# A third weight chunk loaded out of turn, behind packed work buffers, in an encoder block with 32 experts

## The chip, the cores and the metric

The kernel runs on one core of one Trainium2 chip, in one launch. The metric is its time on the device in microseconds, the median of several runs. Beside it stands the hardware profile of one execution, from which all rows below are taken.

## The reference

The reference is one layer of a bidirectional encoder for 256 tokens of width 1024, in float32, cut here to what matters:

```python
h = rms_norm(x, attn_norm_g)                 # attention front
proj = h @ w_in                              # q, k, v of 8 + 12 heads, q of 4 memory heads, 3 gates
merged = gate_a*(A @ w_a) + gate_b*(B @ w_b) + gate_c*(C @ w_c)
x = x + merged @ w_out
h = rms_norm(x, ffn_norm_g)                  # expert part
top_val, top_idx = top_k(h @ router_w + router_b, 4)   # 4 of 32 experts per token
# for each expert, on the tokens that chose it:
gu = xb @ w_gu[e] + b_gu[e]                  # (1024, 2048)
g, u = minimum(gu[:, :1024], 7), clip(gu[:, 1024:], -7, 7)
y = ((u + 1) * g * sigmoid(1.702 * g)) @ w_dn[e] + b_dn[e]   # (1024, 1024)
x = rms_norm(x + sum over the chosen experts of weight * y, final_norm_g)
```

The weights of one expert are 12 MiB, those of all 32 are 384 MiB. All of them are read, whatever the tokens choose.

## The kernel before

**Front.** The weights of the attention part come in 42 chunks of 1 MiB (`NF`) through the first 6 slots of a ring of chunks. Each chunk is split into a high and a low part (ScalarE and GpSimd, `w_parts`), and TensorE (PE) multiplies three pairs of parts. After chunk 41 x is complete; the router's logits, the top 4, the ranks in each expert and the matrices that gather an expert's tokens follow.

**Experts.** One expert is 12 chunks of 1 MiB: 8 of gate and up (k = 0 to 7), 4 of down. Each expert has 64 token slots. PE does, for expert n: the bias rows; the chunks k = 0 to 3; the scatter of expert n-2's result into the four banks that hold x; the turning of the weights; k = 4, 5; a gather of later tokens; k = 6, 7; the four down chunks of expert n-1; the turning of expert n's activation. So the chunks are used in the order gate and up of n, then down of n-1 (`gate_up_chunk`, `down_chunk`, L148 to L155). `chunk_used` counts them. VectorE limits gate and up into `gate_c` and `up_c` (L1492, L1493), multiplies them (L1496, `prod_ready`), multiplies by the sigmoid (L1499), and copies the turned activation (L1501). ScalarE takes the sigmoid of `gate_c` (L1213), and copies the down sums of expert n-1 out of bank 3 into `y_sb` (`move_down`, L1215), which the scatter reads; for the last expert VectorE does this copy (L1513).

**Loads.** All weight loads are issued by SP, in one order. The ring has 20 slots of 8 KB per partition (`RING`, `CHUNK`); chunk c lies in slot (c + 8) mod 20. `TRANSFERS` (L158) groups the chunks: transfers of 2 chunks for the first experts and the last, of 4 for the gate and up chunks of experts 4 to 30, of 2 for the down chunks. A transfer of m chunks from c on is issued when PE has used chunk c - 20 + m - 1 (L534). The first 20 chunks go in before: five transfers during the front (`EARLY_AFTER`), five when the front's last chunks are used (`FIRST_LAP`); the last of these, chunk 16 (down weights of expert 0), waits for all 42 chunks of the front and stands behind four small loads of the expert biases.

**Lent places.** Two chunks of expert 5 (`LENT_TO`), its k = 6 and 7, numbers 62 and 63 (`LENT`), do not go through the ring. They are loaded in pieces of 256 KB into buffers that have become free: x (all of k = 7, since x is by then in the banks), the router's constants, the raw biases, and the routing's scratch (`lent_pieces`, L383). SP issues them between the first lap and the first load of the ring's second lap (L524 to L530, the last piece at L538). They have semaphores of their own (`lent_in`). Their ring slots stay unused in that lap, and the loads after them still wait by their own number. The down bias and the final gain go into x's place when that chunk has been used (L539 to L542), and PE adds the down bias in four matmuls during the experts 9 to 12 (`DOWN_BIAS_AT`).

**Memory.** The front's work buffers and the experts' share one arena behind the ring's first 12 slots, `FRONT_WORK` = 22784 words per partition. The front's parts of the merged tokens (`mergedHL`) lie at its end. The row maxima and the sums of the attention are tensors of their own in front of the arena (L217 to L220).

Of the kernel before, what the change touches and what calls it, by code (L numbers as in the profile page):

```python
# [25 lines left out]
P = 128  # L26
# [13 lines left out]
EXPERTS, TOP_K = 32, 4  # L40
# [7 lines left out]
CHUNK = 2048  # L48
# [3 lines left out]
SCORE_SLOT = 8  # L52
SECOND_SPLIT_SLOT = 10
FRONT_SLOT = 12
FRONT_WORK = 22784
LATE_PARTS = (39, 41)
IMAGES = 3
EXPERT_CHUNKS = 12
# [25 lines left out]
NU = len(UNITS)  # L84
# [8 lines left out]
T5_STORE_AFTER = 11  # L93
STEP_SLOT = {s: i for i, s in STEP_AFTER.items()}

DOWN_BIAS_AT = {9: (0, 0), 10: (0, 1), 11: (1, 0), 12: (1, 1)}
IMAGE_AFTER = {u: 9 if u < 2 + IMAGES else STEP_SLOT[u - IMAGES] + FRONT_RING for u in range(2, NU)}

EARLY_AFTER = {36: 0, 38: 4, 39: 6, 40: 8, 41: 10}
FIRST_LAP = {2: 38, 12: 38, 14: 40, 18: 41, 16: NF}  # L100
FIRST_LONG = 4

LENT_TO = 5
LENT = (EXPERT_CHUNKS * LENT_TO + 2, EXPERT_CHUNKS * LENT_TO + 3)

QK_DONE, QKV_DONE = {"C": 6, "A": 10, "B": 18}, {"C": 6, "A": 12, "B": 21}

# [45 lines left out]
def down_chunk(n):  # L153

    return gate_up_chunk(n + 1) + KC if n + 1 < EXPERTS else EXPERT_CHUNKS * EXPERTS - 4  # L155


def transfers():  # L158

    short, long, down = [(j, 2) for j in range(0, KC, 2)], [(0, 4), (4, 4)], [(KC, 2), (KC + 2, 2)]  # L160
    end_down = [(KC, 2), (KC + 2, 1), (KC + 3, 1)]
    order = [(0, *t) for t in short]
    for n in range(1, EXPERTS):
        lent = [(0, 4), (4, 2), (6, 1), (7, 1)]
        order += [(n, *t) for t in (lent if n == LENT_TO else long if FIRST_LONG <= n < EXPERTS - 1 else short)]
        order += [(n - 1, *t) for t in (down if n < EXPERTS - 1 else end_down)]
    order += [(EXPERTS - 1, *t) for t in end_down]
    c, out = 0, {}
    for e, j, m in order:
        out[c] = (e, j, m)  # L170
        c += m
    return out


TRANSFERS = transfers()


# [4 lines left out]
def build(nc, t):  # L182
# [4 lines left out]
    w_gu = t["expert_w_gate_up"].rearrange("l e (p a) c -> (l e) p (a c)", p=P)  # L187
# [5 lines left out]
    with ExitStack() as ctx:  # L193
        def sb(name, shape, dt=F32):
            return ctx.enter_context(nc.sbuf_tensor(name, shape, dt))
# [13 lines left out]
        until_ranked = sb("until_ranked", [P, 512])  # L209
# [4 lines left out]
        pick_raw = sb("pick_raw", [P, 2, EXPERTS + 1])  # L214
        sumsq = sb("sumsq", [P, 4, T])
        rstd = sb("rstd", [P, 4, T])
        row_max = sb("row_max", [P, NU, 4])  # L217
        neg_max = sb("neg_max", [P, 8, 4])
        exp_sum = sb("exp_sum", [P, NU, 4])
        inv_sum = sb("inv_sum", [P, 8, 4])  # L220
        ovf = sb("ovf", [P, MAX_OVERFLOW + 1], I32)
        b_tmp = sb("b_tmp", [P, 2, 4])

# [2 lines left out]
        FRONT0, MOE0 = FRONT_SLOT * CHUNK, RING * CHUNK  # L226
# [7 lines left out]
        def area(off, *dims):  # L234
            n = int(np.prod(dims))
            assert off + n <= FRONT0 + FRONT_WORK
            flat = arena[:, off:off + n]
            if len(dims) == 2:
                return flat.rearrange("p (a b) -> p a b", a=dims[0])
            if len(dims) == 3:  # L240
                return flat.rearrange("p (a b c) -> p a b c", a=dims[0], b=dims[1])
            if len(dims) == 4:
                return flat.rearrange("p (a b c d) -> p a b c d", a=dims[0], b=dims[1], c=dims[2])
            return flat
# [2 lines left out]
        pT = area(FRONT0, 2, 2, 2, S)  # L247
        image = area(FRONT0 + 2048, IMAGES, 2, IMG)
        na_mask = area(FRONT0 + 2048 + IMAGES * 2 * IMG, 4, GRID_W // 2)
        v = area(FRONT0 + 4352, T, 1280)  # L250
        mv = area(FRONT0 + 6912, T, MEM_HEADS * MEM_HD)
        qkT = area(FRONT0 + 8192, 24, S)
# [32 lines left out]
        place = [MOE0]  # L285

        def moe(*dims):
            at = place[0]
            place[0] += int(np.prod(dims))
            return area(at, *dims)  # L290
# [6 lines left out]
        gate_c, up_c = moe(512), moe(512)  # L297
# [1 line left out]
        assert place[0] <= FRONT0 + 18688  # L299
        router_parts = area(place[0], S)  # L300
        sig = moe(512)
        y_sb, aT = moe(512), moe(4, P)
        wT_sel = moe(S)[0:EXPERTS, :]
        pick = split_at("pick", place[0], 2, 2 * BLK)
        moe(2 * 2 * BLK)
        until_routed = area(place[0], 512)
# [5 lines left out]
        okeys = moe(T, EXPERTS)  # L312
        extra, ends = moe(EXPERTS), moe(EXPERTS)
        ovf_f = moe(MAX_OVERFLOW)
        final_g, far_iota, b_dn = x[:, 0, :], x[:, 1, :], x[0:EXPERTS, 1, :]
        final = xn[:]

# [4 lines left out]
        lent_in = {c: sem(f"lent_in{c}") for c in LENT}  # L322
# [36 lines left out]
        gate_ready, gu_drained, sig_ready = sem("gate_ready"), sem("gu_drained"), sem("sig_ready")  # L359
        prod_ready, act_ready = sem("prod_ready"), sem("act_ready")  # L360
# [16 lines left out]
        def front_fills(r):  # L377
# [2 lines left out]

        x_flat = x[:].rearrange("p t c -> p (t c)")
        bias_flat = bias_raw[:].rearrange("p b c -> p (b c)")
        lent_pieces = {LENT[0]: [bias_flat[:, 0:512], bias_flat[:, 512:1024], until_ranked[:], until_routed],  # L383
                       LENT[1]: [x_flat[:, 512 * i:512 * (i + 1)] for i in range(4)]}

        def piece(c, i):
# [7 lines left out]
        ALL_CHUNKS = EXPERTS * EXPERT_CHUNKS  # L394
# [37 lines left out]
        def _(sp):  # L432
# [13 lines left out]
            for i in range(NF):  # L446
# [7 lines left out]
                kind, n = FRONT[i]  # L454
                dst = ring[:, i % FRONT_RING, :]
                if i in WIDE_FIRST or i in WIDE_LAST:
                    late = int(i in WIDE_LAST)
                    first = (n - late) * SLOTS_W
                    src = {"mem": w_mem, "in": w_in}[kind][:, 4 * late:4 * late + 4, first:first + 2 * SLOTS_W]
                    dst = dst.rearrange("p (k c) -> p k c", k=4)  # L460
                elif kind in ("mem", "in", "out"):
                    src = {"mem": w_mem, "in": w_in, "out": w_out}[kind][:, :, n * SLOTS_W:(n + 1) * SLOTS_W]
                    dst = dst.rearrange("p (k c) -> p k c", k=KC)
                elif kind == "branch_b":
                    src, dst = w_br[kind], dst.rearrange("p (k c) -> p k c", k=2)
                else:
                    src, dst = w_br[kind][:, :, n * 512:(n + 1) * 512], dst.rearrange("p (k c) -> p k c", k=4)
                if i == 0:
                    sp.dma_start(dst[:, 0:KC // 2], src[:, 0:KC // 2]).then_inc(first_half_in, 16)
                    dst, src = dst[:, KC // 2:], src[:, KC // 2:]  # L470
                sp.dma_start(dst, src).then_inc(landed[i % FRONT_RING], 16)
                if i in EARLY_AFTER:
# [6 lines left out]
                    c = EARLY_AFTER[i]  # L479
# [30 lines left out]

            sp.wait_ge(merged_ready, 4)
            sp.dma_start(iota, bass.AP(t["iota"].tensor, 0, [[0, P], [1, BLK]])).then_inc(iota_in, 16)
            for c, used in FIRST_LAP.items():
                sp.wait_ge(chunk_used, used)
                if used == NF:
                    load_bias()
                load_weights(*TRANSFERS[c], ring_slot(c))
            def lend(c, first, n, place):

                e, j, _ = TRANSFERS[c]  # L520
                src = w_gu[bass.ds(e, 1), :, j * CHUNK + 512 * first:j * CHUNK + 512 * (first + n)].rearrange("o p c -> (o p) c")
                sp.dma_start(place, src).then_inc(lent_in[c], 16)

            sp.wait_ge(normed, 3)  # L524
            sp.wait_ge(tile_normed, 1)
# [51 lines left out]
        def _(pe):  # L577
# [345 lines left out]
            def weights_landed(c):  # L923

                if c in LENT:
                    pe.wait_ge(lent_in[c], {LENT[0]: 48, LENT[1]: 16}[c])
                else:
                    pe.wait_ge(landed[ring_slot(c)], 16 * fills_through(c))

# [9 lines left out]
            for n in range(EXPERTS):  # L939
# [10 lines left out]
                for k in range(KC):  # L950
                    c = gate_up_chunk(n) + k
# [47 lines left out]
            with pe.If(0 < n_over):  # L999
                with pe.Fori(0, MAX_OVERFLOW) as b:  # L1000
                    with pe.If(b < n_over):
                        n = b + EXPERTS
# [33 lines left out]
        def _(act):  # L1036
# [68 lines left out]
            for i, (kind, n) in enumerate(FRONT):  # L1105
# [13 lines left out]
                elif kind in ("mem", "in") and i not in WIDE_FIRST:  # L1119
# [5 lines left out]
                    src = ps[:, PLAIN[i] % 2, :].rearrange("p (t c) -> p t c", t=2)  # L1125
                    if kind == "mem":
                        if n < 2:
                            e = nc.scalar.copy(mkT[:, 2 * n:2 * n + 2, :], src)
                        else:
                            e = nc.scalar.copy(mv[:, :, (n - 2) * 256:(n - 1) * 256], src)  # L1130
                    elif n in Q_SCALE and n < 15:

                        e = nc.scalar.mul(qkT[:, QKT[n]:QKT[n] + 2, :].rearrange("p b (t q) -> p b t q", t=T),
                                          reversed_tiles(src), Q_SCALE[n])
                    elif n in QKT:
                        e = nc.scalar.mul(qkT[:, QKT[n]:QKT[n] + 2, :], src, Q_SCALE.get(n, 1.0))
                    elif n in V_COL:
                        e = nc.scalar.copy(v[:, :, V_COL[n]:V_COL[n] + 256], src)
                    else:
                        buf, c = GATE_BRANCH[n]  # L1140
                        e = nc.scalar.activation(gate_cols(buf, c * 256, 256), src, ACT.Sigmoid)
# [9 lines left out]
                if i in STEP_AFTER:  # L1151
# [13 lines left out]
                    if 0 <= u < NU and u == last_unit_of(OUTPUT_OF[u]):  # L1165
                        o = OUTPUT_OF[u]
                        act.wait_ge(pv_done, u + 1)
                        high, _, src = output_parts(o)
# [43 lines left out]
                act.wait_ge(gate_ready, n + 1)  # L1212
                nc.scalar.activation(sig, gate_c, ACT.Sigmoid, scale=ALPHA).then_inc(sig_ready, 1)  # L1213

            def move_down(chunks, bank):  # L1215
                act.wait_ge(chunk_used, chunks + NF)
                nc.scalar.copy(y_sb, ps[:, bank, :]).then_inc(y_ready, 1)  # L1217

            for n in range(EXPERTS):
                if n:  # L1220
                    move_weights(n - 1, (n - 1) % 2)
                if n + 2 < EXPERTS:
                    move_gathered(n % 2, XT[:, (n // 2 + 1) % 2], 2 * BLK, n + 2)
                sigmoid(n)
                if n:
                    move_down(down_chunk(n - 1) + 4, 3)
            move_weights(EXPERTS - 1, (EXPERTS - 1) % 2)
            n_over = act.value_load(ovf[0:1, MAX_OVERFLOW:MAX_OVERFLOW + 1], min_val=0, max_val=MAX_OVERFLOW)
            with act.If(0 < n_over):
                with act.Fori(0, MAX_OVERFLOW) as b:  # L1230
                    with act.If(b < n_over):
                        for half in range(2):
                            move_gathered(half, XT[:, 0], BLK, b * 2 + (EXPERTS + half))
                        move_weights(b + EXPERTS, 1)
                        sigmoid(b + EXPERTS)
                        move_down(b * EXPERT_CHUNKS + (ALL_CHUNKS + EXPERT_CHUNKS), 3)

            nc.scalar.activation(b_tmp[:, 0, 0:1], eps[:], ACT.Sqrt)
            for tt in range(T):
# [367 lines left out]
```

## Time and profile before

| | us |
|---|---|
| median of 3 runs | 1232.18 (1231.66 to 1232.54) |
| profiled execution: its own time | 1229.89 |
| profiled execution: span | 1228.1 |
| PE busy | 1174.6 (96%) |
| VectorE busy | 267.5 (22%) |
| ScalarE busy | 253.0 (21%) |
| GpSimd busy | 207.2 (17%) |
| bytes moved by DMA | 455.14 MB, mean 371 GB/s |

The span is the time from the first to the last instruction of the profiled execution. The share of busy time is a mean over the whole span, which has a front of some 305 us and an expert part of some 920 us with different limits, so it has to be read in stretches. Matmuls are pipelined and their ends are modelled: a busy PE may still wait a little inside.

### The profile page before, as it was taken

What the parts mean: (1) busy time and instruction counts of PE and PEld (TensorE: products, weight loads), DVE (VectorE), ACT (ScalarE), POOL (GpSimd) and SP (SyncE); (2) the same over time, 40 slices, a digit from 0 to 9 for tenths busy, and PEclk for the clock granted to TensorE, in tenths of its full rate; (3) what the DMA queues carried; (4) which work ended last, traced back from release to release, by engine and by line L of the source; (5) the groups of instructions that cost most, each with busy time, mean ns of one, the idle gap of its engine ahead of it and who ended that gap; (6) DMA issues with size and microseconds to landing.
All of it is one profiled execution on the core that took longest, in us unless ns stands there. A gap on an engine that the chain in (4) does not pass through costs nothing.

```text
span 1228.1 us, 14301 instructions
## 1 busy us (share of the span) xinstructions
PE 1174.6 (96%) x6225; PEld 605.9 (49%) x6225; DVE 267.5 (22%) x543; ACT 253.0 (21%) x531; POOL 207.2 (17%) x89
## 2 busy tenths in 40 slices
PE   8999999999999999999999999999998998999996
PEld 8989887899433433333333333333333333333332
DVE  3148252232411112111111121111111111111112
ACT  6446455344301011100101010000100000000101
POOL 5865766686100000000000000000000000000000
PEclk9999999999999999999999999999999999999999
DMA  9753544599999999999999999999999999999995
GB/s 316 241 168 122 167 155 137 185 357 389 347 428 430 425 430 415 430 430 429 432 432 431 428 430 431 430 429 430 433 429 431 427 432 428 430 429 427 430 427 231
DMA packets 61703, 455.14 MB, mean 371 GB/s; under 512 B 5081, under 2 KB 33657, under 8 KB 43464
## 3 DMA queue, kind: packets, MB, share of 16 engines
q1 hardware_dynamic: 61640, 454.22, 90.0%
q8 instruction: 50, 0.82, 0.3%
q14 instruction: 13, 0.11, 0.0%
HBM read 453.13 MB, written 1.07 MB: 370 GB/s over the span
## 4 chain that ended last, share of the span: by engine, by line
PE 63%; DMA 33%; DVE 1%; POOL 1%; ACT 1%; issue 0%; DVEq 0%; SPq 0%; ACTq 0%; POOLq 0%
PE ps L579 62%; DMA arena<-in_expert_w_gate_up 29%; DMA arena<-in_expert_w_down 3%; POOL w_parts L568 1%; PE ps L895 1%; PE ps L889 0%; DVE arena L1371 0%; DMA arena<-in_mem 0%; DVE x_normed L1542 0%; PE ps L702 0%; PE ps L586 0%; ACT arena L1087 0%; PE ps L679 0%; DVE arena L1401 0%; DVE arena L1267 0%
## 5 line engine op out<-in xcount | busy, mean ns | idle before, releaser
L579 PE MATMUL ps<-arena,gathered_T 128*64 128x512 f32 x2034 | 471.2, 611 | 36.3 <-DMA arena<-in_expert_w_gate_up 36.3
L579 PE MATMUL ps<-arena 128*64 128x512 f32 (+8 forms) x1650 | 335.7, 534 | 4.1 <-DVE arena L1401 1.6
L579 PEld LDWEIGHTS ps<-arena,gathered_T 128*64 128x64 f32 x2034 | 144.9, 140 | 302.0 <-issue 273.3
L579 PEld LDWEIGHTS ps<-arena 128*64 128x64 f32 (+3 forms) x1650 | 132.2, 153 | 198.9 <-issue 191.6
L568 POOL TENSOR_TENSOR w_parts<-arena,w_parts 128x1024 fp32r<-128x1024 f32 x42 | 102.9, 2474 | 46.8 <-ACT w_parts L1067 37.7
L568 POOL TENSOR_TENSOR w_parts_odd<-arena,w_parts_odd 128x1024 fp32r<-128x1024 f32 x38 | 90.8, 2409 | 45.7 <-ACT w_parts_odd L1067 45.7
L1486 DVE TENSOR_SCALAR arena<-arena 128x128 f32<-128x128 f32 x64 | 19.3, 344 | 315.3 <-PE ps L889 315.3
L1209 ACT COPY arena<-ps 128x256 f32<-128x256 f32 x32 | 11.9, 372 | 358.8 <-PE ps L889 358.8
L1492 DVE TENSOR_SCALAR arena<-ps 128x512 f32<-128x512 f32 x32 | 22.1, 692 | 273.1 <-PE ps L579 273.1
L579 PEld LDWEIGHTS ps<-arena,x_normed 128*128 128x128 f32 x512 | 59.5, 192 | 24.8 <-issue 24.3
L1200 ACT ACTIVATE gathered_T<-ps,g_cols 128x128 f32<-128x128 f32 x128 | 36.5, 368 | 170.1 <-PE ps L579 170.1
L579 PE MATMUL ps<-arena,x_normed 128*128 128x128 f32 x512 | 65.4, 281 | 0.2 <-DVE arena L1443 0.2
L579 PE MATMUL ps<-w_parts_odd,h_T_parts 128*128 128x256 f32 (+1 forms) x360 | 59.1, 322 | 0.0
L1501 DVE COPY arena<-ps 128x512 f32<-128x512 f32 x32 | 22.1, 691 | 155.1 <-PE ps L895 155.1
L579 PEld LDWEIGHTS ps<-w_parts_odd,h_T_parts 128*128 128x128 f32 x360 | 51.5, 188 | 7.1 <-issue 1.8
L1217 ACT COPY arena<-ps 128x512 f32<-128x512 f32 x31 | 18.2, 586 | 172.3 <-PE ps L579 172.3
L1067 ACT CAST w_parts<-arena 128x1024 fp32r<-128x1024 f32 x40 | 39.9, 1047 | 49.2 <-PE ps L579 49.0
L1067 ACT CAST w_parts_odd<-arena 128x1024 fp32r<-128x1024 f32 x38 | 37.9, 1047 | 40.8 <-PE ps L579 40.3
L1213 ACT ACTIVATE arena<-arena 128x512 f32<-128x512 f32 x32 | 20.3, 633 | 109.6 <-DVE arena L1492 109.6
L579 PE MATMUL ps<-w_parts,h_T_parts 128*128 128x512 f32 (+1 forms) x216 | 41.1, 347 | 0.0
L579 PEld LDWEIGHTS ps<-w_parts,h_T_parts 128*128 128x128 f32 x216 | 33.7, 188 | 6.2 <-issue 0.6
L579 PE MATMUL ps<-h_T_parts,w_parts 128*128 128x256 f32 x288 | 35.5, 282 | 0.0
(181 smaller groups left out, 727.1 us busy)
## 6 DMA issues: line engine op xcount, KB each, us to landing
arena<-in_expert_w_gate_up SPq DMA_DIRECT2D x53, 4096.0 KB, 39.4
arena<-in_expert_w_down SPq DMA_DIRECT2D x62, 2048.0 KB, 38.8
arena<-in_expert_w_gate_up SPq DMA_DIRECT2D x21, 2048.0 KB, 12.4
arena<-in_w_in SPq DMA_DIRECT2D x29, 1024.0 KB, 5.4
arena<-in_w_out SPq DMA_DIRECT2D x4, 1024.0 KB, 11.3
arena<-in_expert_w_down SPq DMA_DIRECT2D x4, 1024.0 KB, 41.0
arena<-in_w_mem_kv SPq DMA_DIRECT2D x3, 1024.0 KB, 12.3
arena<-in_w_branch_a SPq DMA_DIRECT2D x2, 1024.0 KB, 5.1
```

Source lines behind the costliest of these rows:

```text
L568: last = nc.gpsimd.tensor_tensor(parts_at(i)[:, 1, half], ring[:, i % FRONT_RING, half], parts_at(i)[:, 0, half].bitcast(F32), ALU.subtract)
L579: return nc.tensor.matmul(out, lhsT, rhs, start=start, stop=stop, **kw)
L895: last = nc.tensor.transpose(ps[:, 2, f * P:(f + 1) * P], sig.rearrange("p (q f) -> p f q", f=4)[:, f, :], ident[:])
L1067: nc.scalar.copy(parts_at(i)[:, 0, half], ring[:, i % FRONT_RING, half]).then_inc(high_ready, 1)
L1200: last = nc.scalar.mul(xt[:, c, 0:width], ps[:, bank, k * P:k * P + width], g_cols[:, 3 * KC + c:3 * KC + c + 1])
L1209: nc.scalar.copy(WT[:, wt_slot, :], ps[:, 3, 0:S]).then_inc(WT_ready, 1)
L1213: nc.scalar.activation(sig, gate_c, ACT.Sigmoid, scale=ALPHA).then_inc(sig_ready, 1)
L1217: nc.scalar.copy(y_sb, ps[:, bank, :]).then_inc(y_ready, 1)
L1486: last = vec.tensor_scalar(PW[:, tt, :].rearrange("p (a s) -> p a s", a=2), bcast(slots, 1, 2), key_tile[:, tt, e], w_sel[:, tt, e], ALU.i ...
L1492: vec.tensor_scalar(gate_c, ps[:, 0, :], LIMIT, None, ALU.min).then_inc(gate_ready, 1)
L1501: vec.tensor_copy(aT, ps[:, 2, :].rearrange("p (f s) -> p f s", f=4)).then_inc(aT_ready, 1)
```

## The change

A third chunk is lent. All three belong to expert 6, the seventh (k = 5, 6 and 7, numbers 73 to 75), and expert 5 gets all its chunks through the ring. The new one, `LENT[2]` (k = 7), is one transfer of 1 MiB into a place of its own, the last 2048 words of the arena (`behind_work`), and is issued right behind chunk 16, before SP's waits for the normed tokens. Chunk k = 4 of expert 6 is then a ring transfer of one chunk.

To make room, the arena grows by 240 words, the four tiles of row maxima and sums move into a gap of it (between the mask and the values), and the down sums `y_sb` take the buffer of `gate_c`. ScalarE's copy of the down sums waits in addition for `prod_ready` and `sig_ready`. The load of the down bias and the final gain, and its additions, move one expert later.

```diff
-FRONT_WORK = 22784
+FRONT_WORK = 23024
...
-DOWN_BIAS_AT = {9: (0, 0), 10: (0, 1), 11: (1, 0), 12: (1, 1)}
+DOWN_BIAS_AT = {10: (0, 0), 11: (0, 1), 12: (1, 0), 13: (1, 1)}
...
-LENT_TO = 5
-LENT = (EXPERT_CHUNKS * LENT_TO + 2, EXPERT_CHUNKS * LENT_TO + 3)
+LENT_TO = 6
+LENT = tuple(EXPERT_CHUNKS * LENT_TO + j for j in (1, 2, 3))
...
-        lent = [(0, 4), (4, 2), (6, 1), (7, 1)]
+        lent = [(0, 4), (4, 1), (5, 1), (6, 1), (7, 1)]
...
-        row_max = sb("row_max", [P, NU, 4])
-        neg_max = sb("neg_max", [P, 8, 4])
-        exp_sum = sb("exp_sum", [P, NU, 4])
-        inv_sum = sb("inv_sum", [P, 8, 4])
...
+        stats_at = FRONT0 + 4096
+        row_max, exp_sum = area(stats_at, NU, 4), area(stats_at + 64, NU, 4)
+        neg_max, inv_sum = area(stats_at + 128, 8, 4), area(stats_at + 192, 8, 4)
...
-        y_sb, aT = moe(512), moe(4, P)
+        y_sb, aT = gate_c, moe(4, P)
...
+        behind_work = area(FRONT0 + FRONT_WORK - CHUNK, CHUNK)
+        assert place[0] <= FRONT0 + FRONT_WORK - CHUNK
...
-        lent_pieces = {LENT[0]: [bias_flat[:, 0:512], bias_flat[:, 512:1024], until_ranked[:], until_routed],
+        lent_pieces = {LENT[2]: [behind_work[:, 512 * i:512 * (i + 1)] for i in range(4)],
+                       LENT[0]: [bias_flat[:, 0:512], bias_flat[:, 512:1024], until_ranked[:], until_routed],
...
             for c, used in FIRST_LAP.items():
                 sp.wait_ge(chunk_used, used)
                 if used == NF:
                     load_bias()
                 load_weights(*TRANSFERS[c], ring_slot(c))
+            lend(LENT[2], 0, 4, behind_work)
 
             sp.wait_ge(normed, 3)
...
-                    pe.wait_ge(lent_in[c], {LENT[0]: 48, LENT[1]: 16}[c])
+                    pe.wait_ge(lent_in[c], {LENT[0]: 48, LENT[1]: 16, LENT[2]: 16}[c])
...
-            def move_down(chunks, bank):
+            def move_down(chunks, bank, n):
                 act.wait_ge(chunk_used, chunks + NF)
+                act.wait_ge(prod_ready, n + 1)
+                act.wait_ge(sig_ready, n + 1)
                 nc.scalar.copy(y_sb, ps[:, bank, :]).then_inc(y_ready, 1)
```

## Rows read from the trace of the kernel before

**Rows 1.** The page, rate of all DMA engines in 40 slices of 30.7 us:

```profile
GB/s 316 241 168 122 167 155 137 185 357 389 347 428 430 425 430 415 430 430 429 432 432 431 428 430 431 430 429 430 433 429 431 427 432 428 430 429 427 430 427 231
```

**Rows 2.** Busy by windows: length, PE, PEld, DVE, ACT, POOL, PEclk, DMA share, GB/s.

```profile
324.00:650.00 326.00, 324.61 (x1566) 125.09 (x1564) 53.72 (x122) 34.62 (x88) 0.00 (x0) 1.00 1.01 428
650.00:1200.00 550.00, 513.30 (x2398) 196.04 (x2394) 82.70 (x183) 49.65 (x125) 0.00 (x0) 0.98 1.00 429
...
1200.00:1221.00 21.00, 19.06 (x86) 6.96 (x86) 3.65 (x6) 3.83 (x8) 0.00 (x0) 1.00 0.57 237
```

**Rows 3.** Waits of PE, in total: us, times, longest.

```profile
PE ps L579 <- DMA arena<-in_expert_w_gate_up: 36.3, 27, 2.8
...
PE ps L579 <- DMA arena<-in_expert_w_down: 1.3, 1, 1.3
```

**Rows 4.** The chain of waits that ended last: start, length, what.

```profile
440.19 0.68 PE ps L895 x4
...
466.66 0.68 PE ps L895 x4
...
649.30 37.10 DMA arena<-in_expert_w_gate_up
...
1160.60 40.15 DMA arena<-in_expert_w_down
...
1211.01 7.04 PE ps L579 x32
```

**Rows 5.** Timeline of SP, 285 to 350 us: start, length, DMA issued.

```profile
307.27 0.58 SPq L440 DMA_DIRECT2D arena<-in_expert_w_down  x1
313.76 0.33 SPq L522 DMA_DIRECT2D x_tokens<-in_expert_w_gate_up  x1
...
315.95 0.33 SPq L522 DMA_DIRECT2D bias_raw<-in_expert_w_gate_up  x1
321.51 0.33 SPq L440 DMA_DIRECT2D arena<-in_expert_w_gate_up  x1
```

**Rows 6.** Busy time by windows, around the added transfer.

```profile
307.00:314.00 7.00, 6.86 (x31) 3.74 (x30) 4.56 (x27) 5.21 (x6) 3.85 (x1) 1.00 1.00 341
...
314.00:322.20 8.20, 8.15 (x54) 5.18 (x56) 7.41 (x28) 2.28 (x8) 0.00 (x0) 1.00 0.64 240
```

**Rows 7.** Time to landing of the loads issued at 313.8, 315.9, 321.5, 380.4, 459.8.

```profile
DMA to landing us min/median/max: 4.8/4.8/4.8
...
DMA to landing us min/median/max: 4.9/4.9/4.9
...
DMA to landing us min/median/max: 7.1/7.1/7.1
...
L440 SPq DMA_DIRECT2D arena<-in_expert_w_gate_up x1: 328/328/328, 380.4 to 380.4; - x1
...
DMA to landing us min/median/max: 13.8/13.8/13.8
...
L440 SPq DMA_DIRECT2D arena<-in_expert_w_gate_up x1: 328/328/328, 459.8 to 459.8; - x1
...
DMA to landing us min/median/max: 18.6/18.6/18.6
```

**Rows 8.** Timeline near the end, ScalarE's copy and who waits.

```profile
1201.72 0.69 DVE L1499 TENSOR_TENSOR arena<-arena 128x512 f32<-128x512 f32 x1
...
1208.01 0.59 ACT L1217 COPY arena<-ps 128x512 f32<-128x512 f32 x1 [7.06 <-PE ps L579]
1208.65 0.30 PEld L579 LDWEIGHTS ps<-arena 64*128 64x128 f32 x4 [0.18 <-ACT arena L1217]
```

**Rows 9.** Timeline of PE: products behind a wait.

```profile
1098.03 7.09 PE L579 MATMUL ps<-arena,gathered_T 128*64 128x512 f32 x32 [2.35 <-DMA arena<-in_expert_w_gate_up]
...
1127.30 8.78 PE L579 MATMUL ps<-arena,gathered_T 128*64 128x512 f32 x32 [2.38 <-DMA arena<-in_expert_w_gate_up]
...
1200.89 7.09 PE L579 MATMUL ps<-arena 128*64 128x512 f32 x32 [1.33 <-DMA arena<-in_expert_w_down]
```

More of the change, by code:

```diff
@@ L512, in _, with lend @@
             sp.dma_start(iota, bass.AP(t["iota"].tensor, 0, [[0, P], [1, BLK]])).then_inc(iota_in, 16)
+            def lend(c, first, n, place):
+                e, j, _ = TRANSFERS[c]
+                src = w_gu[bass.ds(e, 1), :, j * CHUNK + 512 * first:j * CHUNK + 512 * (first + n)].rearrange("o p c -> (o p) c")
+                sp.dma_start(place, src).then_inc(lent_in[c], 16)
             for c, used in FIRST_LAP.items():
@@ L517, in _ @@
                 load_weights(*TRANSFERS[c], ring_slot(c))
[L518 to L522, printed above, removed]
+            lend(LENT[2], 0, 4, behind_work)
             sp.wait_ge(normed, 3)
@@ L1225, in _ @@
                 if n:
-                    move_down(down_chunk(n - 1) + 4, 3)
+                    move_down(down_chunk(n - 1) + 4, 3, n)
             move_weights(EXPERTS - 1, (EXPERTS - 1) % 2)
@@ L1235, in _ @@
                         sigmoid(b + EXPERTS)
-                        move_down(b * EXPERT_CHUNKS + (ALL_CHUNKS + EXPERT_CHUNKS), 3)
+                        move_down(b * EXPERT_CHUNKS + (ALL_CHUNKS + EXPERT_CHUNKS), 3, b + EXPERTS)
             nc.scalar.activation(b_tmp[:, 0, 0:1], eps[:], ACT.Sqrt)
```

## The prediction

> **What bounds the kernel now.** I read the page first. In its line of GB/s the rate is 122 to 389 in the first eleven slices (each is 30.7 us), the attention front and the routing; from the twelfth on it stays between 415 and 433, up to the last slice [rows 1]. The table by windows makes that exact: 428 GB/s at a DMA share of 1.01 from 324 to 650 us, 429 GB/s at 1.00 from 650 to 1200 us [rows 2]. So the weights of 32 experts come in one unbroken stream that begins at about 322 us. Whether this stream also sets the time is told by PE's waits: on weights of gate and up it waited 36.3 us, on weights of down 1.3 us [rows 3], and the chain of waits shows from when. Up to 649.30 us it is all PE: two successive turns of an activation stand at 440.19 and 466.66 us, so PE has a period of 26.47 us per expert, in which it frees 12 chunks. One expert of 12 MiB takes the stream 12 x 1.0486 MB / 429 GB/s = 29.3 us. PE is the quicker by 2.9 us per expert, uses up what had been loaded ahead, and from 649.30 us on the long pieces of the chain are DMA, the last of them from 1160.60 to 1200.75 us [rows 4]. What is left is PE work of fixed length: the last down products but one at 1200.89 us [rows 9], the last at 1211.01 to 1218.05 us. The end is thus the landing of expert 30's first down chunks plus some 27 us, and that landing is set by how many bytes the stream has to bring before it, since it never pauses.
>
> Two consequences. PE work before 1200 us costs nothing up to the 37.6 us that it waits. And a byte is worth its time only if it leaves the stream: it has to be moved to a time at which the queues stand empty.
>
> **The added transfer.** A third chunk of 1 MiB is taken out of the stream (72 to 75 of expert 6: one in the ring, three lent; before, two of expert 5) and is loaded by SP right behind the last load of the first lap, before SP's wait for the normed tokens. At 429 GB/s it is worth 1,048,576 / 429,000 = 2.44 us.
>
> Is there an empty place for it? The last load of the first lap (2 MiB of down weights) is issued at 307.27 us; then SP sleeps until 313.76 us, issues the lent pieces until 316.3 us, sleeps again until routing is done enough and issues the first ring load behind the lap at 321.51 us [rows 5]. The 16 DMA engines are full from 307 to 314 us (share 1.00), but from 314 to 322.2 us their share is 0.64 at 240 GB/s [rows 6]: 8.2 x 0.36 = 2.95 us of all engines stand idle, or, by bytes, (429 - 240) x 8.2 = 1.55 MB against the 1.05 MB to be put there. The new transfer would be issued at about 307.9 us and lie ready behind the 2 MiB; the pieces issued at 313.76 us and later follow it. All is done about half a microsecond before 322.2 us, when the data of the 321.51 load start. That load is released by PE (chunks 0 and 1 of expert 0 used), so it neither comes earlier nor later. I take the whole 2.44 us as hidden. The bounds: nothing hidden (the gain is 0), all hidden (2.44 us).
>
> Here the Trainium skill speaks against the change: "DMA: Bandwidth & Descriptors", section "Bandwidth", gives a transfer of 1 MB 6.15 us and 341 GB/s, and its "Anatomy of one DMA" a fixed part of about 2 us for each. By that an estimate of the new transfer is 4.4 to 6.2 us, which is 1.5 to 3.2 us more than the idle 2.95, and the sum would be between a gain of 0.9 us and a loss of 0.8 us. The trace disagrees for transfers that stand behind each other: 1 MiB issued at 313.76 us landed after 4.8 us and the 0.5 MiB issued at 315.95 us landed by 320.9 us [rows 5, 7], so three transfers with 1.75 MiB took 7.1 us in all, where three fixed parts of 2 us and the bytes would be 10.3.
>
> **The later skip.** A lent chunk leaves a hole in the ring's order: the next load still waits until PE has used the chunk 20 before it. In the hole nothing is issued, and the queue is eaten by so much. If it runs dry, the gain is lost there. The depth ahead of a transfer follows from its time to landing. On an empty queue 2 MiB took 7.1 us, of which 4.9 are bytes, so 2.2 are start and receipt. The 4 MiB issued at 380.42 us took 13.8: less 9.8 for its bytes and 2.2, 1.8 us of work stood ahead of it, and the stream did not pause. The 4 MiB issued at 459.83 us took 18.6: 6.6 us stood ahead [rows 7]. In the new kernel expert 5 brings all of its 8 gate and up chunks through the ring (2 MiB more than before, issued by 414 us), expert 6 brings 5 (3 MiB less, by 435 us). So up to the hole the queue is deeper than before, and at 459.83 us, its least, shallower by 1 MiB: 6.6 - 2.44 = 4.2 us, more than twice what sufficed at 380 us. From there PE frees chunks 2.9 us per expert faster than they arrive, and the depth grows. Cost of the skip: 0, with bounds 0 and the 6.6 us in which PE frees three chunks (3/12 of 26.47).
>
> The loads of the down bias and the final gain move one expert later with the x buffer, and so do the four additions of the bias (experts 10 to 13). These 0.6 MiB are in the full stream either way: 0. PE's additions fall before 649 us or into its slack: 0. The number of ring transfers is the same for the experts 5 and 6 together (four). SP issues one DMA more, 0.33 us in a sleep of 5.9 us [rows 5]: 0.
>
> **The moved buffers.** The four tiles of row maxima and sums go behind the work buffers of the front into a gap between the mask and the values; no wait is added, and the transfers that overwrite this place already wait for the attention's end: 0.
>
> The down sums take the buffer of the gate. ScalarE's copy then waits for two more semaphores: the product that reads the gate (VectorE) and the sigmoid. Queued behind the copy on ScalarE are the next weights' copy and gather, and PE's scatter waits for it. The product is long done: in the last expert the activation product that follows it starts at 1201.72 us, and the copy at 1208.01, 6.3 us later [rows 8]. Only the passing of two satisfied waits is left. Nearly everywhere that is hidden (the scatter comes after four chunks of products, 7.1 us [rows 9]), but once it isn't: at 1208.65 us PE's weight load for the second last scatter is released by this copy [rows 8], and all that follows is on the path. The nearest row: the activation product, which has two waits, starts 0.04 us after the product before it ended. So 0 to 0.1 us; I take 0.05.
>
> **Sum.** -2.44 + 0.05 = -2.39 us. The profiled execution took 1229.89 us for a span of 1228.1; the new one would take 1227.5. The runs' median is 1232.18, 2.3 us above that execution; taken as the same in both kernels, the forecast is 1229.8 us, with a scatter like that of the three runs (0.9 us from end to end). What can be told from no change here is about 0.2%, 2.46 us: the forecast lies almost on that line.
>
> **Rivals.**
> A. The transfer isn't hidden: it delays what comes behind it, and the stream starts later by what it takes out. For it: 2.95 us of room for 2.44, in scraps, of which only the end is truly empty. If the start and receipt of 2.2 us [rows 7] were paid by each transfer in the queue, it would take 4.6 us, 1.7 more than the room, and the time would be 1229.8 + 1.7 = 1231.5; with nothing hidden at all, 1232.2. (The skill's fixed part of 2 us, from the page and section above, is the rule for this case.) Against it: the three transfers of 7.1 us, and that even a small overrun meets no one, as the data of the next load start only at 322.2. Chance 0.11.
> B. The queue runs dry in the hole of three chunks, and the kernel is slower. Place: 435 to 460 us, where SP waits for PE to use the chunks 20 before. Price: each dry microsecond is one of the end, at most the 6.6 us of three chunks, so up to 1232.2 + 4.2 = 1236.4; slower than before from 2.44 dry us on. For that the depth of 4.2 us would have to be overrated by 6.6 us. Against it: 1.8 us sufficed at 380 us. Chance 0.05, with 1234 as its middle.
> C. The clock. After a wait of 2.35 us at 1098.03 the 32 products took 7.09 us, after one of 2.38 at 1127.30 they took 8.78, with half the granted clock for part of them [rows 9]: 1.69 us. Before 1200 us that sits in PE's slack. If it falls behind 1200 us, where the granted clock was 1.00 until PE's last product [rows 2], 0.7 us of the gain is left: 1231.5. The last wait before it is shorter, 1.33 us [rows 9], so 0.06.
> D. More than forecast: short stretches of the stream below its mean close with a deeper queue between 414 and 433 us. 1229.0, chance 0.03.
> The forecast has the other 0.75.
>
> **How the numbers follow.** The likeliest case alone spans 1229.2 to 1230.4. The range goes down to 1229.0, and up to 1231.8, which takes in C and most of A. Faster by over 0.2% needs 1229.72 or less: a little under half of the forecast's 0.75 and D, 0.40. Slower by over 0.2%: B and the scatter of A and C, 0.07. Within 0.2%: 0.53.
>
> **What would show it.** Right: from 314 to 322 us the DMA share rises from 0.64 to about 0.95, and the load of 321.51 us is issued and landed as before; the chain up to 640 us keeps its times to 0.1 us; the 4 MiB issued near 459.8 us lands about 2.4 us sooner after its issue (some 16.2 us), and no stretch between 435 and 500 us falls under its neighbours; PE waits about 35 us on weights; the last down products but one start near 1198.5 us. Wrong: the 321.51 load lands later (A), a gap in the GB/s near 460 us (B), a granted clock below 1 behind 1198 us (C), a scatter that starts more than 0.1 us behind its turned activations (the shared buffer).

## The result and the profile after

The changed kernel took 1223.4 us (median of 4 runs, 1221.93 to 1224.31) against 1231.92 us of before on the same count: a ratio of 0.9932, 95% interval 0.9918 to 0.9947. That is 8.5 us less, where 2.4 had been forecast; 1223.4 lies far below the range's lower end of 1229.0. The profiled execution took 1221.93 us with a span of 1220.1.

First the steps that came as forecast. In the timeline of SP after, the new load stands behind the first lap, and the ring's second lap begins 12.6 us later (start, length, DMA issued):

```profile
307.77 0.43 SPq L519 DMA_DIRECT2D arena<-in_expert_w_gate_up  x1
312.60 0.33 SPq L519 DMA_DIRECT2D x_tokens<-in_expert_w_gate_up  x1
...
320.35 0.33 SPq L442 DMA_DIRECT2D arena<-in_expert_w_gate_up  x1
```

By windows, after (length, PE, PEld, DVE, ACT, POOL, PEclk, DMA share, GB/s):

```profile
314.00:322.20 8.20, 8.20 (x51) 4.45 (x51) 6.32 (x25) 2.29 (x8) 0.00 (x0) 1.00 0.98 384
...
324.00:650.00 326.00, 324.61 (x1568) 125.10 (x1568) 55.72 (x124) 35.32 (x89) 0.00 (x0) 1.00 1.01 430
650.00:1200.00 550.00, 517.32 (x2423) 196.82 (x2418) 83.05 (x183) 49.74 (x125) 0.00 (x0) 0.98 1.00 431
```

The empty place is filled: from 314 to 322.2 us the DMA share rose from 0.64 to 0.98 [rows 6]. The second lap's first load landed 7.3 us after its issue, against 7.1 before [rows 7], so here the new transfer delayed nothing. But the two lines under it hold what was not forecast. The stream runs at 430 and 431 GB/s, not 428 and 429 [rows 2], at the same share of 1.01 and 1.00: the engines are as busy as before and move more in the same time.

The chain of waits of after (start, length, what):

```profile
439.00 0.68 PE ps L899 x4
...
465.47 0.68 PE ps L899 x4
...
701.06 37.97 DMA arena<-in_expert_w_gate_up
...
1152.90 39.87 DMA arena<-in_expert_w_down
```

PE's period is 26.47 us as in [rows 4], so PE's expert work is untouched. Its long DMA pieces begin at 701 us, two expert periods later than the 649 of before, and the last ends at 1192.77 instead of 1200.75. The 8.0 us between them split so: the ring's second lap begins 1.16 us earlier (320.35 against 321.51 us, [rows 5]), though nothing of the front was meant to be faster; the chunk is 2.44 by its bytes; what is left is 4.4 us, and the rate accounts for about that: the stretch without the chunk is 877 us, and 877 x (431/429 - 1) = 4.1 us.

PE's waits on weights, in total (us, times, longest):

```profile
PE ps L583 <- DMA arena<-in_expert_w_gate_up: 31.4, 27, 3.2
...
PE ps L583 <- DMA arena<-in_expert_w_down: 1.3, 1, 1.3
```

The queue at its least depth, the 4 MiB issued at 458.6 us:

```profile
L442 SPq DMA_DIRECT2D arena<-in_expert_w_gate_up x1: 328/328/328, 458.6 to 458.6; - x1
...
DMA to landing us min/median/max: 14.8/14.8/14.8
```

14.8 less 9.8 and 2.2 is 2.8 us of work ahead of it. It was 6.6 before [rows 7], and 4.2 had been forecast; more than the 1.8 us that sufficed at 380 us.

The shared buffer, ScalarE's copy and PE's weight load behind it in the timeline near the end:

```profile
1200.03 0.59 ACT L1223 COPY arena<-ps 128x512 f32<-128x512 f32 x1 [7.00 <-PE ps L583]
1200.67 0.30 PEld L583 LDWEIGHTS ps<-arena 64*128 64x128 f32 x4 [0.19 <-ACT arena L1223]
```

The weight load starts 0.64 us after the copy starts, and before it did so too [rows 8]; its idle time is 0.19 us against 0.18. The two waits cost no more than 0.01 us here.

So a rate and a front that got better have to be explained. One edit had been priced as nothing: the four small tiles that left their place in front of the arena. The arena is laid behind the fixed tensors, rounded to 64 bytes, so it moved down by their 640 bytes: from byte 39552 of each partition, which is 128 past a multiple of 256, to 38912, which is a multiple. Every slot of the ring is 8192 bytes, so the rows of every weight transfer into the ring moved with it. So did all work buffers in the arena.

### The profile page after: what moved, and what is told of

Same layout as the page of the kernel before. It is cut to its first block, busy times and chain, and to the rows that moved or that the text cites. A ratio compares the mean times of both kernels' runs of the same rounds, so it can differ in the third digit from the quotient of the medians.

```text
span 1220.1 us, 14333 instructions
## 1 busy us (share of the span) xinstructions
PE 1171.6 (96%) x6225; PEld 603.3 (49%) x6225; DVE 263.3 (22%) x543; ACT 253.4 (21%) x531; POOL 207.6 (17%) x89
## 4 chain that ended last, share of the span: by engine, by line
PE 66%; DMA 30%; DVE 1%; POOL 1%; ACT 1%; issue 0%; DVEq 0%; SPq 0%; ACTq 0%; POOLq 0%
PE ps L583 64%; DMA arena<-in_expert_w_gate_up 26%; DMA arena<-in_expert_w_down 3%; POOL w_parts L572 1%; PE ps L899 1%; PE ps L893 1%; DVE arena L1377 0%; DMA arena<-in_mem 0%; DVE x_normed L1548 0%; PE ps L706 0%; PE ps L590 0%; ACT arena L1091 0%; PE ps L683 0%; DVE arena L1407 0%; DVE arena L1273 0%
```

## The experiments

All times are medians of 5 to 11 runs, each set with before beside it (1231.27, 1230.82 and 1230.35 us in the three sets). The first set has `stats_aligned`, `stats_old_place`, `after_plus128` and `after_plus256`, the second `before_plus128`, `after_plus64`, `no_third` and `third_late`, the third the other four. A difference between two kernels of five runs each is uncertain by some 1.5 us.

**The tiles moved, nothing else** (`stats_aligned`: the arena at 38912). Its edit to the kernel before:

```diff
-        row_max = sb("row_max", [P, NU, 4])
...
+        stats_at = FRONT0 + 4096
+        row_max, exp_sum = area(stats_at, NU, 4), area(stats_at + 64, NU, 4)
...
```

> The kernel before with one thing changed: the four tiles of row maxima and sums moved into the arena's gap, so that the arena begins 640 bytes lower in each partition, at byte 38912 instead of 39552 (0 instead of 128 past a multiple of 512 bytes). No third chunk, no shared buffer. Theory of the place (the streams' destinations are better aligned, so the DMA rate rises from 429 to 431 GB/s, and the front gets 1.1 us shorter): 5 to 6 us faster than before, 1226 to 1227 us, 431 GB/s from 650 to 1200 us. Theory of the chunk (all of the gain comes with the third chunk): same as before, 1232 us, 429 GB/s.

Measured: 1224.99 us, ratio 0.9954 (0.9941 to 0.9967), 6.3 us less than before. Its stream behind 510 us:

```profile
510.00:1150.00 640.00, 608.40 (x2866) 233.79 (x2862) 100.06 (x224) 60.71 (x155) 0.00 (x0) 0.98 1.00 432
```

The kernel before, same window:

```profile
510.00:1150.00 640.00, 606.53 (x2852) 233.27 (x2850) 99.69 (x224) 61.08 (x157) 0.00 (x0) 0.98 1.00 430
```

That is a little more than the 5 to 6 us expected, and about three quarters of the gain, without the chunk that the change was made for.

**The tiles moved, the arena at its old byte** (`stats_old_place`):

```diff
-        base = -(-nc.sbuf_base // 64) * 64
+        base = -(-nc.sbuf_base // 64) * 64 + 640
```

> The same as stats_aligned, but 640 bytes are left empty in front of the arena, so that it begins at byte 39552 as in the kernel before. Theory of the place: as before, 1232 us, 429 GB/s. Theory that the small tiles' move itself matters (other neighbours for VectorE and ScalarE): as fast as stats_aligned.

Measured: 1231.8 us, ratio 1.0004 (0.9995 to 1.0012), and the rate is back at 430:

```profile
510.00:1150.00 640.00, 604.60 (x2848) 232.83 (x2846) 99.17 (x223) 61.25 (x157) 0.00 (x0) 0.98 1.00 430
```

It is the arena's byte, not the tiles' new place, that brings the gain.

**The kernel before, one constant changed** (`before_plus128`: the arena at 39680):

```diff
-        base = -(-nc.sbuf_base // 64) * 64
+        base = -(-nc.sbuf_base // 64) * 64 + 128
```

> The kernel before with one constant changed: the arena begins 128 bytes higher (39680, a multiple of 256 bytes, where before it lay 128 past one). Nothing else. Theory of the place (destinations at multiples of 256 bytes): as stats_aligned, 1225 us, some 6 us faster than before; 431 GB/s in the stream, and the front's products with w_parts as the moving operand 281 ns instead of 282. Rival (the low address, or the tiles gone from in front of the arena, bring it): 1231 to 1232 us, as before.

Measured: 1225.15 us, ratio 0.9957 (0.9943 to 0.9970), 5.7 us less than before.

```profile
510.00:1150.00 640.00, 611.22 (x2865) 234.53 (x2861) 100.02 (x224) 60.72 (x155) 0.00 (x0) 0.98 1.00 432
```

The arena is higher here than in the kernel before, and the tiles are where they were, so it is neither the low address nor the tiles.

**The changed kernel, moved by 128, 256 and 64 bytes.** The edit is the one above with + 128, + 256 or + 64, and `FRONT_WORK = 22960`, which takes unused room away.

> The changed kernel with the arena 128 bytes higher (39040, that is 128 past a multiple of 512, as before had it), 64 words less of unused room at its end, all else the same. Theory of the place: the third chunk's 2.4 us stay, the 5 to 6 us go: 1228.5 to 1229.8 us. Theory of the chunk: 1223.4 us as after.

> The changed kernel with the arena 256 bytes higher (39168, 256 past a multiple of 512). If the transfers want multiples of 256 bytes: 1223.4 us as after. If they want multiples of 512 bytes: as with 128, 1228.5 to 1229.8 us. Theory of the chunk: 1223.4 us too.

> The changed kernel with the arena at 38976, 64 bytes past a multiple of 256. If each row that begins off a multiple of 256 bytes is cut at its ends in the same way, wherever it begins: as after_plus128, 1229.7 us. If what counts is how far off it is, or only halves of 256 bytes: another time, above it (twice the loss, 1235 us) or below it (1224 to 1227 us).

Measured: 1229.68 us with 128 (ratio 0.9987, 0.9978 to 0.9995), 1223.45 with 256 (0.9937, 0.9925 to 0.9948), 1228.86 with 64 (0.9981, 0.9972 to 0.9990). In this order, their streams:

```profile
510.00:1150.00 640.00, 608.03 (x2870) 234.28 (x2870) 100.06 (x224) 61.97 (x159) 0.00 (x0) 0.98 1.00 430
```

```profile
510.00:1150.00 640.00, 608.64 (x2876) 233.56 (x2872) 100.73 (x225) 61.90 (x158) 0.00 (x0) 0.98 1.00 432
```

```profile
510.00:1150.00 640.00, 609.49 (x2864) 234.05 (x2861) 100.02 (x224) 60.80 (x155) 0.00 (x0) 0.98 1.00 430
```

The gain goes with 128 and with 64 bytes, to nearly the same time, and is whole with 256; from 128 to 256, in one set, it is 6.2 us. So multiples of 256 bytes are what counts, not of 512. All kernels of this study agree: 432 GB/s in this window for the nine whose arena begins at a multiple of 256, 430 for the four where it doesn't. The bytes moved in the window are finer than these rounded rates. The kernel before and `before_plus128`:

```profile
DMA packets 12618, 275.02 MB, mean 430 GB/s; under 512 B 1394, under 2 KB 1394, under 8 KB 1394
```

```profile
DMA packets 12666, 276.33 MB, mean 432 GB/s; under 512 B 1402, under 2 KB 1402, under 8 KB 1402
```

The four off the boundary moved 274.99 to 275.05 MB (275.02 with 64 bytes, 275.05 with 128), the nine on it 276.17 to 276.46: 0.47% more on average, with no overlap. There are as many packets per MB, so a row is not cut into more of them; each takes longer. By an estimate from the lines above, 16 engines x 640 us / packets is 811.5 against 808.5 ns, 3 ns for each.

With the arena off, what is left of the change against before is 1.6 us (128 bytes) and 2.0 us (64), where 2.4 had been forecast: this is the change without its unforeseen part.

The Trainium skill has a rule in this direction. "DMA: Bandwidth & Descriptors", section "How a descriptor splits into AXI transactions", says that for a descriptor that does not start at a multiple of 256 bytes the first transaction starts at the boundary below, and that the bytes before the start are fetched for nothing and still cost bus beats. The runs agree with the boundary, and not with a price that goes by the bytes before the start: 64 and 128 bytes off cost the same rate. The Trainium skill tells this of reads; here the source in HBM was left alone, and of the transfers' two sides only the one that writes on chip moved. But the engines' operands in the arena moved with it, and no run moved the ring alone. PE's period per expert stayed at 26.47 us, so nothing points at the engines; that it is the writing side is argued, not shown.

**The front.** Its 1.1 us are partly PE's. Products of the split tokens (`h_T_parts`) and a split weight, before and after (busy us, mean ns of one | idle before). The row names the moving operand first, so here it is the tokens, and the split weight, which lies in the arena, is the one that is loaded; the expectations of `before_plus128` have this the wrong way round:

```profile
L579 PE MATMUL ps<-h_T_parts,w_parts 128*128 128x256 f32 x288 | 35.5, 282 | 0.0
```

```profile
L583 PE MATMUL ps<-h_T_parts,w_parts 128*128 128x256 f32 x288 | 35.2, 281 | 0.0
```

It is 0.3 us here. The same group with the odd weights (288 products) lost 0.3 too, and one in which the weight is the moving operand (240 products) 0.4. The three busy times of after came back in the profiles of `stats_aligned`, `before_plus128`, `no_third`, `after_plus256` and `after_again` within 0.1 us. The time of the second lap's first load follows the byte less well: 320.35 to 320.94 us in eight of the ten profiles with the arena on a multiple of 256, but 321.71 in `after_plus256` and 322.04 in `all_aligned`; off it 320.98 (`after_plus64`), 321.51, 321.70 and 323.65. So the front's 1.1 us are seen in single profiles, and not in all. Whether aligning the tokens too gives more was the question of `all_aligned`, the changed kernel with the fixed tensors in another order:

```diff
+        g_cols = sb("g_cols", [P, 4 * KC])
         ident = sb("ident", [P, P])
         g_rows = sb("g_rows", [4 * KC, P])
-        g_cols = sb("g_cols", [P, 4 * KC])
-        eps = sb("eps", [P, 1])
         x = sb("x_tokens", [P, T, D])
...
         until_ranked = sb("until_ranked", [P, 512])
+        eps = sb("eps", [P, 1])
```

> The changed kernel with the fixed tensors in another order, so that x, the normed x, the split tokens (h_T_parts) and the router's constants begin at multiples of 256 bytes too (before: 32 past one). Theory of the place, for DMA: x and the constants take 1.75 MiB of 454 MB by DMA, so nothing is gained in the stream. For PE, whose products in the front read these tiles: if its reads also want multiples of 256 bytes, up to another 1 us from the front, 1222.4 us; if not, 1223.4 us.

Measured: 1223.5 us, no gain over the changed kernel. These products even got slower, while two groups of 120 products with 512 columns got faster (29.2 to 28.6 us each). So PE's part is no matter of multiples of 256:

```profile
L583 PE MATMUL ps<-h_T_parts,w_parts 128*128 128x256 f32 x288 | 36.1, 285 | 0.0
```

**The chunk alone** (`no_third`: the changed kernel with `LENT_TO = 5`, two lent chunks and no load into `behind_work`, and the changed kernel run once more, `after_again`, which came in the next set and not beside it).

> The changed kernel without the third chunk: two chunks lent to the sixth expert as before; the arena's place, the moved tiles, the shared buffer and the two added waits as in the changed kernel. Theory (a chunk of 1 MiB out of a full stream is 2.4 us, the shared buffer costs at most 0.1 us): 1225 to 1226 us, 2.4 us over the changed kernel, and the same as stats_aligned within 0.2 us. Rival (part of the chunk's worth is lost in the early place or the hole): 1.0 to 1.6 us over the changed kernel. If the shared buffer's waits cost more than 0.1 us, no_third is above stats_aligned by as much.

> The changed kernel once more, unchanged, beside the others of this set: 1223.4 us, 1.7 us under no_third.

Measured: 1225.15 and 1223.35 us. The chunk is worth 1.8 us by these two, or 1.3 if each is taken against before in its own set; 1.5 between `stats_aligned` and `after_plus256`, in one set; 1.6 and 2.0 with the arena off. Forecast were 2.4. Taken together, 15 runs of three kernels with two lent chunks and 20 of four with three, arena in place, each less the mean of before in its set, differ by 1.8 us, give or take 0.8. So it is probably less than forecast, but 2.4 is inside that.

Single profiles show where some of it can go. From the issue of the second lap to PE's first product on expert 30's down weights, three kernels with two lent chunks took 875.8 us on average (874.6 to 876.8) and four with three took 872.6 (872.4 to 872.7) with the arena in place, a difference of 3.2; with it off, 879.5 and 877.7, two each, a difference of 1.8. The second lap's first load landed after 7.1 to 7.5 us in the seven profiles without a third chunk in the early place. With one there it was 7.2 to 7.4 us in four, but 8.5 in `after_plus128`, 9.7 in `after_plus64` and 9.5 in `three_to_sixth`. In these three the early transfers ran over into the second lap, which is rival A's sign. The mean of the seven is 8.1, some 0.9 us late, enough for the missing part of the 2.4; with one profile of each kernel that is a fit and not a proof.

`no_third` is equal to `before_plus128` of its set (both 1225.15 us), which has neither the moved tiles nor the shared buffer, so these cost nothing that can be told.

**When it is loaded.** `third_late` issues it at some 330 us, `third_at_60` at 413 us:

```diff
-            lend(LENT[2], 0, 4, behind_work)
...
+                if c == RING + 4:        # third_at_60: if c == 60
+                    lend(LENT[2], 0, 4, behind_work)
```

> The changed kernel with the same third chunk, loaded later: issued behind the third load of the ring's second lap (some 330 us), where the queues are full, and not behind the first lap at 308 us. Theory (its gain is that it fills an empty place): the gain goes, 1225.5 to 1226 us, as no_third. Rival (what counts is that the chunk is ahead of its turn, whenever): 1223.4 us as the changed kernel.

> The changed kernel with the third chunk loaded just behind chunk 60 (some 413 us), where 4 to 5 MiB stand in the queue, and still two expert periods before its use. third_late (at 330 us) kept about 1.2 us of the chunk's gain. Theory: it kept them because with a queue of 1 MiB single DMA engines run empty for moments until some 400 us, and one more MiB in it closes these; then at 413 us nothing is left to close: 1225.1 us, as no_third. Rival (a chunk ahead of its turn is worth something whenever it is loaded): 1223.5 to 1224.0 us.

Measured: 1223.96 and 1224.8 us. At 330 us it is 1.2 us under `no_third` of the same set, where the theory had expected no gain; at 413 us it is 1.45 us over `after_again` of the same set. Neither is clear of noise (the runs of each pair overlap). The stretch from the second lap's issue to expert 30's down products says the same: 872.4 to 872.7 us with the chunk in the empty place, 874.1 at 330 us, 874.7 at 413 us, 874.6 in `no_third`. So a chunk loaded ahead of its turn into a full queue looks worth next to nothing, and the empty place is what pays. That a shallow queue leaves single engines empty until some 400 us, and one more MiB in it helps, fits the two times; it was argued from them and not measured by itself.

**Where the hole is** (`three_to_sixth`: `LENT_TO = 5` with three chunks).

> The changed kernel with all three lent chunks given to the sixth expert (61, 62, 63) and not the seventh; the down bias one expert earlier again. Theory of the hole: before, 2.9 us of work stood ahead of the load issued at 433 us (14.9 us to landing, less 9.8 and 2.2); with a hole of three chunks 0.5 us are left there, so the queues run partly empty at 430 to 434 us and 0.5 to 1.5 us of the chunk's worth are lost: 1224.0 to 1225.0 us. If the place of the hole does not matter: 1223.4 us.

Measured: 1224.44 us, 1.1 us over `after_again`, as the theory of the hole had it. But with five runs each (1223.38 to 1225.41 and 1222.07 to 1225.80 us) it is not clear of noise. The 4 MiB issued in the hole:

```profile
L442 SPq DMA_DIRECT2D arena<-in_expert_w_gate_up x1: 327/327/327, 432.8 to 432.8; - x1
...
DMA to landing us min/median/max: 13.3/13.3/13.3
```

1.3 us stood ahead of it, the least seen at a 4 MiB load. The stream of this kernel, and of the changed one, over the shallow part:

```profile
322.00:500.00 178.00, 176.61 (x858) 68.15 (x856) 29.83 (x65) 19.47 (x48) 0.00 (x0) 1.00 1.00 424
```

```profile
322.00:500.00 178.00, 176.61 (x858) 67.86 (x852) 29.84 (x65) 19.48 (x48) 0.00 (x0) 1.00 1.01 429
```

424 against 429 GB/s in 178 us would be 2 us in these two executions. But the windows of 2 us at the hole do not show the empty queue that the theory had there:

```profile
430.00:432.00 2.00, 2.00 (x12) 0.70 (x10) 0.00 (x0) 0.32 (x2) 0.00 (x0) 1.00 0.99 426
432.00:434.00 2.00, 2.00 (x12) 0.72 (x10) 1.23 (x2) 0.50 (x1) 0.00 (x0) 1.00 1.04 410
434.00:436.00 2.00, 2.00 (x14) 0.58 (x10) 1.45 (x3) 0.13 (x1) 0.00 (x0) 1.00 1.08 434
```

And this execution was late well before: its first load of the second lap, issued at 320.9 us, landed after 9.5 us, where `after_again` had 7.2:

```profile
L442 SPq DMA_DIRECT2D arena<-in_expert_w_gate_up x1: 328/328/328, 320.9 to 320.9; - x1
...
DMA to landing us min/median/max: 9.5/9.5/9.5
```

So whether a hole at the sixth expert costs anything stays open. Rival B's mechanism was not shown.

## Why the prediction was wrong

**What bounds the kernel: right.** The stream of weights sets the end, and PE's period is the same 26.47 us. From PE's first product on expert 30's down weights to the end it is 27.2 us in twelve of the fourteen profiles; in `three_to_sixth` (28.0) and `after_plus64` (28.6) PE waited once more, for that expert's last chunks.

**The added transfer: right in its place, probably too high in its size.** In the changed kernel's profile it was hidden (share 0.64 to 0.98, second lap not delayed), but in three of the seven profiles that have it there the next load landed 1.3 to 2.5 us late. It brought 1.3 to 2.0 us by medians instead of 2.4, which the noise does not exclude. The fixed part of about 2 us for each transfer, which the prediction took from the Trainium skill ("DMA: Bandwidth & Descriptors", "Anatomy of one DMA"), is told there of transfers issued from GpSimd. For these, issued from SP behind each other, it did not come up as a loss of that size.

**The later skip: right.** No loss at the seventh expert was seen, though the depth of 2.8 us was less than the 4.2 forecast. One expert earlier the time was 1.1 us longer, which is not clear of noise and not traced to the hole.

**The shared buffer: right.** At most 0.01 us in the profile where 0.05 was taken, and nothing in the medians.

**The moved buffers: here it failed.** The step said: "no wait is added, and the transfers that overwrite this place already wait for the attention's end: 0." It asked what the four tiles meet in their new place, and not what stood behind them in the old one. The arena's first byte went from 128 past a multiple of 256 to a multiple, and all weights of the experts but the lent pieces outside the arena land by that byte. Measured by `before_plus128` and `stats_aligned`, the term put at 0 is 5.7 and 6.3 us: 0.47% of rate over 877 us (4.1 us), some 1.1 us in the front where the profiles show it, and 0.5 to 1.1 us that neither places.

The sum with the measured terms is -5.7 to -6.3 for the arena's byte and -1.3 to -2.0 for the chunk: -7.0 to -8.3, against the measured -8.5 with an interval of 6.5 to 10.1. None of the rivals had this: D, more than forecast, was given 0.03 and stopped at 1229.0.

## What to carry to other kernels

Where a kernel is bound by its DMA stream, work out the byte at which each large destination begins, before and after an edit: a small tensor taken away in front of it moves it. Round the base up to 256 bytes, not 64; here that one constant was worth about three times the chunk for which buffers were packed. Bytes taken out of a stream pay where the queues are empty, and an empty place that just holds them may not hold them in every execution. Before opening a hole in the ring's order, ask how deep the queue ahead of it is: the time to landing, less bytes and receipt, tells it.

## What the runs showed of the hardware

With the arena, and so the rows of the transfers into its ring, beginning 64 or 128 bytes past a multiple of 256, a full stream of HBM to SBUF ran at 430 GB/s instead of 432, at an unchanged share of busy DMA engines and with as many packets per MB; 64 and 128 bytes cost the same rate (275.02 and 275.05 MB in 640 us, against 276.17 to 276.46) and nearly the same time (1228.86 and 1229.68 us), and a multiple of 256 that is none of 512 costs nothing (1223.45 us). PE's products in the front changed their mean by 1 to 5 ns with the bytes at which their operands lie (281, 282 and 285 ns for 256 columns, 398 and 393 ns for 512), not in step with multiples of 256.
